# Nine residual chunks turned by VectorE block transposes and DMAs instead of TensorE

## What is computed

```python
def residual_update(x, out, g_post, p_i, w_pp, w_pg):
    x = x + rms_norm(out, g_post)
    return x + (p_i @ w_pp) * jax.nn.sigmoid(x @ w_pg)

def first_block(...):
    out = mixer_a(rms_norm(x, norm_pre[0]), w_in_a[0], w_out_a[0])
    x = residual_update(x, out, norm_post[0], p[0], w_ple_proj[0], w_ple_gate[0])
    kv = shared_kv(x, kv_norm, w_dkv, ...)
    out = mixer_b(rms_norm(x, norm_pre[1]), kv, w_in_b[0], ...)
    return residual_update(x, out, norm_post[1], p[1], w_ple_proj[1], w_ple_gate[1])

def hybrid_layer(h, ...):
    proj = rmsnorm(h, norm1_w) @ w_in
    ...
    h = h + mixed @ w_out
    z = rmsnorm(h, norm2_w) @ mlp_w1
    return h + jnp.square(jax.nn.relu(z)) @ mlp_w2
```

## Time and profile before

| what | us |
|---|---|
| median of 3 runs | 2087.79 |
| lowest and highest run | 2087.12, 2089.4 |
| span of the profiled execution | 2088.3 |
| TensorE matmuls busy in it | 2076.1 |
| VectorE, ScalarE busy in it | 1228.3, 1067.9 |
| GpSimd busy in it | 6.1 |

### The profile page before, as it was taken

One profiled execution on the slowest core, in us unless ns is written; L12 is line 12 of the kernel. 1 busy time (PEld: TensorE's weight loads), 2 busy tenths in 40 slices (PEclk: granted clock), 3 DMA queues, 4 the chain that ended last, 5 costly groups with the idle time before them and its releaser, 6 DMA issues.

```text
span 2088.3 us, 27247 instructions
## 1 busy us (share of the span) xinstructions
PE 2076.1 (99%) x10904; PEld 1779.2 (85%) x10904; DVE 1228.3 (59%) x1506; ACT 1067.9 (51%) x1478; POOL 6.1 (0%) x12
## 2 busy tenths in 40 slices
PE   9999999999999999999999999999999999999998
PEld 8888888888898888888889988888888888888887
DVE  5555556556567767646545557555545645655655
ACT  6444566645566565545564345454434434434443
POOL 0000000000000000000000000000000000000000
PEclk9999999999999999999999999999999999999999
DMA  7666555555556544565545446566666566566664
GB/s 253 187 183 192 178 151 155 188 189 178 189 166 190 159 141 154 177 193 183 187 142 158 136 138 206 184 188 187 195 192 189 190 196 189 187 195 187 192 192 150
DMA packets 211100, 375.16 MB, mean 180 GB/s; under 512 B 13843, under 2 KB 48885, under 8 KB 210582
## 3 DMA queue, kind: packets, MB, share of 16 engines
q1 hardware_dynamic: 210982, 373.52, 57.7%
HBM read 371.38 MB, written 2.10 MB: 179 GB/s over the span
## 4 chain that ended last, share of the span: by engine, by line
PE 99%; ACT 0%; DMA 0%; SPq 0%; DVE 0%; issue 0%; ACTq 0%
PE acc L500 20%; PE acc L502 20%; PE acc L501 20%; PE acc L1023 6%; PE acc L597 3%; PE xb L1023 3%; PE tp L1023 3%; PE acc L1026 3%; PE tp L512 2%; PE acc L916 2%; PE acc L917 2%; PE acc L918 2%; PE tp L597 1%; PE xb L597 1%; PE acc L600 1%; PE tp L1026 1%
## 5 line engine op out<-in xcount | busy, mean ns | idle before, releaser
L1585 DVE TENSOR_TENSOR wlo<-raw,whi 128x1024 fp32r<-128x1024 f32 (+1 forms) x650 | 789.7, 1218 | 704.3 <-ACT whi L1080 703.5
L1080 ACT ACTIVATE whi<-raw 128x1024 fp32r<-128x1024 f32 (+1 forms) x650 | 684.6, 1055 | 789.3 <-PE acc L502 470.2
L500 PE MATMUL acc<-whi,ahi 128*128 128x512 f32 (+1 forms) x976 | 377.9, 387 | 0.0
L502 PE MATMUL acc<-whi,alo 128*128 128x512 f32 (+1 forms) x976 | 374.5, 384 | 0.0
L501 PE MATMUL acc<-wlo,ahi 128*128 128x512 f32 (+1 forms) x976 | 374.0, 383 | 0.0
L500 PEld LDWEIGHTS acc<-whi,ahi 128*128 128x128 f32 x976 | 183.2, 188 | 36.6 <-issue 2.7
L502 PEld LDWEIGHTS acc<-whi,alo 128*128 128x128 f32 x976 | 183.2, 188 | 36.5
L501 PEld LDWEIGHTS acc<-wlo,ahi 128*128 128x128 f32 x976 | 183.4, 188 | 34.3
L1023 PE MATMUL acc<-bT,whi 128*128 128x512 f32 x512 | 160.8, 395 | 0.0
L500 PE MATMUL acc<-whi,bhi 128*128 128x512 f32 x384 | 150.5, 392 | 0.0
L502 PE MATMUL acc<-whi,blo 128*128 128x512 f32 x384 | 149.5, 389 | 0.0
(11 more groups left out here) (366 smaller groups left out, 3089.8 us busy)
## 6 DMA issues: line engine op xcount, KB each, us to landing
raw<-in_mlp_w SPq DMA_DIRECT2D x256, 512.0 KB, 4.3
raw<-in_w_in_a SPq DMA_DIRECT2D x128, 512.0 KB, 4.2
raw<-in_w_ple_gate SPq DMA_DIRECT2D x64, 512.0 KB, 4.4
raw<-in_w_in SPq DMA_DIRECT2D x64, 512.0 KB, 3.8
raw<-in_w_in_b SPq DMA_DIRECT2D x40, 512.0 KB, 4.0
raw<-in_w_out_a SPq DMA_DIRECT2D x32, 512.0 KB, 4.2
raw<-in_w_out_b SPq DMA_DIRECT2D x32, 512.0 KB, 4.4
raw<-in_w_out SPq DMA_DIRECT2D x32, 512.0 KB, 4.4
```

Source lines behind the costliest of these rows:

```text
L500: pe.matmul(o, hi[:, kt, tok], whi[:, slot, wc], start=start, stop=False)
L502: mm = pe.matmul(o, lo[:, kt, tok], whi[:, slot, wc], start=False, stop=stop)
L1080: act.activation(whi[:, u % RING, 0:n], raw[:, u % RING, 0:n], ACT.Copy).then_inc(hi_done, 1)
L1585: dve.tensor_tensor(wlo[:, u % RING, 0:n], raw[:, u % RING, 0:n], whi[:, u % RING, 0:n].bitcast(F32), ALU.subtract).then_inc(lo_done, 1)
```

## The change

Chunks 0 to 2 of x2, x4 and x5 are no longer turned by TensorE. The table `ALONG` is gone. Instead:

1. After the addition that finishes a chunk, VectorE waits for it and turns its 32x32 blocks, each within its 32 partitions, with two transposes of 128x512 (`blocks_turned`, L1676), into the half of `stg` that it has just read, under the name `blk`.
2. SP moves the blocks to their partitions by 16 DMAs of 32 KB (32 partitions, 2 rows of 512 bytes each) from `blk` into the new 4 KB buffer `mov` (`move_blocks`). They stand in four groups of four, behind the loads of step 7 of the next chunk and of the three units after it (`MOVE_AT`). Ahead of the first of a chunk SP waits for `blocks`, and for `split_lo` of the chunk before, since there is only one `mov`.
3. At step 6 of the following chunk ScalarE waits for all 16 (`moved`) and rounds `mov` to the high half (`hi_moved`), one instruction of 1024 or four of 256 with a gain; VectorE makes the low half (`lo_moved`).
4. TensorE waits for `split_lo` instead of `tp_done` where it reads these chunks (`operands`).

The last chunks (batches 6 and 7) stay with TensorE.

```diff
-ALONG = {1: {5: [0, 1]}, 2: {5: [2, 3]}, 3: {5: [4, 5]}}
+BLK = 32
+TURNED_BY = {"x2": "gate0", "x4": "gate1", "x5": "out2"}
+MOVED = [(name, c) for name in TURNED_BY for c in range(3)]
...
+        mov = sb("mov", [P, TT, P // BLK, QT, BLK], F32, region(4 * KB))
+        blk = [sb(f"blk{i}", [P, TT, P // BLK, QT, BLK], F32, stg_at + i * 4 * KB) for i in range(2)]
...
+        MOVE_AT = {S[TURNED_BY[name]].u0 + 8 * (c + 1) + 7 + q: (n, q) for n, (name, c) in enumerate(MOVED) for q in range(P // BLK)}
...
                 sp.dma_start(dst, unit_source(s, j, uu)).then_inc(raw_full[u % RING], 16)
+                if isinstance(j, int) and u in MOVE_AT:
+                    move_blocks(*MOVE_AT[u])
+
+            def move_blocks(n, q):
+                if q == 0:
+                    sp.wait_ge(sem("blocks"), n + 1)
+                    if n:
+                        sp.wait_ge(sem("split_lo"), n)
+                for i in range(P // BLK):
+                    sp.dma_start(mov[q * BLK:(q + 1) * BLK, :, i].rearrange("a t f b -> a t (f b)"),
+                                 blk[block_par(n)][i * BLK:(i + 1) * BLK, :, q].rearrange("a t f b -> a t (f b)")).then_inc(sem("moved"), 16)
...
+            def hi_moved(name, c, dst, gain=None):
+                act.wait_ge(sem("moved"), 256 * (MOVED.index((name, c)) + 1))
+                src = mov[:, :].rearrange("p t i f b -> p f (t i) b")
+                to = dst[:, QT * c:QT * (c + 1), :].rearrange("p f (i b) -> p f i b", b=BLK)
+                ...
+                m.then_inc(sem("split_hi"), 1)
...
+            def blocks_turned(name, c):
+                par = block_par(MOVED.index((name, c)))
+                for t in range(TT):
+                    m = dve.transpose(blk[par][:, t].rearrange("p j f b -> p f j b"),
+                                      x[:, t, c * CH:(c + 1) * CH].rearrange("p (f j b) -> p f j b", f=QT, j=P // BLK))
+                m.then_inc(sem("blocks"), 1)
...
                     dve.tensor_tensor(x[:, :, cols], x[:, :, cols], pp[:, :, cols], ALU.add).then_inc(x_done, 1)
+                    if j < 3:
+                        dve.wait_ge(x_done, 8 * layer + 4 + j + 1)
+                        blocks_turned(x2, j)
...
                 dve.tensor_tensor(x1, x1, acc[p][1][:, :], ALU.add).then_inc(evac_dve, 1)
+                if j < 3:
+                    dve.wait_ge(evac_dve, c + 1)
+                    blocks_turned("x5", j)
...
-                along(S["out2"], j, los("x5", x5hi, x5lo, GC["norm2"], ALONG[j]) if j else los("mixed", ahi, alo, mixed_gain, MIXED_LATE))
+                along(S["out2"], j, {6: [lambda j=j: lo_moved("x5", j - 1, x5hi, x5lo, GC["norm2"])]} if j else los("mixed", ahi, alo, mixed_gain, MIXED_LATE))
```

More of the change, by code:

```diff
@@ L287, in build @@
         x_done = sem("x_done")
-        order = [("gcol", 1), ("x0", 8), ("p", 2), ("norms", 1), ("ogA", 8), ("x1", 8), ("x2", 8), ("ckv", 2), ("kr", 1),
-                 ("cq", 2), ("uq", 16), ("ogB", 8), ("x3", 8), ("x4", [0, 1, 2, 3, 4, 5]), ("meta", 1),
+        order = [("gcol", 1), ("x0", 8), ("p", 2), ("norms", 1), ("ogA", 8), ("x1", 8), ("x2", [6, 7]), ("ckv", 2), ("kr", 1),
+                 ("cq", 2), ("uq", 16), ("ogB", 8), ("x3", 8), ("meta", 1),
                  ("x4", [6, 7]), ("rsb", 1), ("qdec", 2), ("kend", 2),
-                 ("vT", 4), ("kvM", 1), ("mixed", 8), ("x5", 8)]
+                 ("vT", 4), ("kvM", 1), ("mixed", 8), ("x5", [6, 7])]
         whole = ("gcol", "norms", "kr", "uq", "rsb", "qdec", "kend", "vT", "kvM")
@@ L486, in product, with operands @@
                     if need:
-                        pe.wait_ge(tp_done, BATCH[need, uu][0] + 1)
+                        operands(need, uu)
                     unit(u + uu, bank, hi, lo, uu * s.kt, s.kt, s.cols, uu == 0, uu == s.units - 1, r)
+            def operands(name, uu):
+                if (name, uu // 2) in MOVED:
+                    pe.wait_ge(sem("split_lo"), MOVED.index((name, uu // 2)) + 1)
+                else:
+                    pe.wait_ge(tp_done, BATCH[name, uu][0] + 1)
             def unit(u, bank, hi, lo, kt0, n, cols, first, last, r=0):
@@ L708, in post @@
                 for j in range(4):
-                    hooks = turns(x2, ALONG[j]) if j else turns(x1, X1_LATE)
+                    hooks = {} if j else turns(x1, X1_LATE)
                     if layer and j == 3:
@@ L986, in _ @@
             for j in range(4):
-                product(S["out2"], j, ahi, alo, need=None if j else "mixed", hooks=turns("x5", ALONG[j]) if j else turns("mixed", MIXED_LATE))
+                product(S["out2"], j, ahi, alo, need=None if j else "mixed", hooks={} if j else turns("mixed", MIXED_LATE))
             def up(q, j):
@@ L1122, in hi_batch @@
                 m.then_inc(tp_hi, 1)
+            def hi_moved(name, c, dst, gain=None):
+                act.wait_ge(sem("moved"), 256 * (MOVED.index((name, c)) + 1))
+                src = mov[:, :].rearrange("p t i f b -> p f (t i) b")
+                to = dst[:, QT * c:QT * (c + 1), :].rearrange("p f (i b) -> p f i b", b=BLK)
+                if gain is None:
+                    m = act.activation(to, src, ACT.Copy)
+                else:
+                    for k in range(QT):
+                        g = gain + QT * c + k
+                        m = act.activation(to[:, k], src[:, k], ACT.Copy, scale=gcol[:, g:g + 1])
+                m.then_inc(sem("split_hi"), 1)
             def squares(norm, j, src, junk=None):
@@ L1307, in last_squares @@
                         squares(norms, j - 1, x)
-                    hooks = join({4: [last_squares]}, his(x2, x4hi if layer else ahi, gain, ALONG[j])) if j else his(x1, ahi if layer else bhi, None, X1_LATE)
+                    hooks = join({4: [last_squares]}, {6: [lambda j=j: hi_moved(x2, j - 1, x4hi if layer else ahi, gain)]}) if j else his(x1, ahi if layer else bhi, None, X1_LATE)
                     along(s, j, join(hooks, {6: [meta_in], 7: [meta_root]}) if layer and j == 3 else hooks)
@@ L1628, in lo_batch, with lo_moved @@
                 m.then_inc(tp_done, 1)
+            def blocks_turned(name, c):
[4 more added lines that the diff above has]
+                m.then_inc(sem("blocks"), 1)
+            def lo_moved(name, c, hi, lo, gain=None):
+                dve.wait_ge(sem("split_hi"), MOVED.index((name, c)) + 1)
+                src = mov[:, :].rearrange("p t i f b -> p f (t i) b")
+                from_hi, to = (a[:, QT * c:QT * (c + 1), :].rearrange("p f (i b) -> p f i b", b=BLK) for a in (hi, lo))
+                if gain is None:
+                    m = dve.tensor_tensor(to, src, from_hi.bitcast(F32), ALU.subtract)
+                else:
+                    for k in range(QT):
+                        g = gain + QT * c + k
+                        m = dve.scalar_tensor_tensor(out=to[:, k], in0=src[:, k], scalar=gcol[:, g:g + 1], in1=from_hi[:, k].bitcast(F32),
+                                                     op0=ALU.mult, op1=ALU.subtract)
+                m.then_inc(sem("split_lo"), 1)
             def copy_batch(name, f, dst, r=0):
```

9 lines of the change are left out of this document (6 added, 3 removed).

## The result

The changed kernel takes **2101.65 us** (median of 4 runs, 2099.89 to 2102.91) where the kernel before takes 2087.78 beside it: ratio 1.0067, 95% interval 1.0053 to 1.0080. It is 13.9 us slower; 7.8 us faster was forecast, and the range ended at 2086.0. Its profiled execution spans 2098.1 us (in every run shown here the time is the span plus 1.8).

A forecast was written before the change was run, and what follows sets the result against it. TensorE, busy 2076.1 of 2088.3 us, was taken as the bound: 2088.3 - 8.1 for the removed transposes + 0.3 for a stall at q2 = 2080.5, less 0.5 from span to median: 2080.0 us, range 2078.5 to 2086.0.

The forecast's parts named there:

- Nine groups at 0.90 us: On TensorE: nine groups of 8 transposes removed, each adding 0.89 to 0.90 us to a chunk, 8.1 us saved.
- Rival 3: On VectorE: block transposes of 4-byte data run at a quarter of the rate, 2.76 us each; 2094.4 us, chance 0.04.
- rival 4: On the DMA engines: moves are served one after another, 1.7 us each, costing 148 us; 2228 us, chance 0.01.
- rival 5: TensorE wasn't the bound, and the 8.1 us turn into waits for weight splits; 2087.8 us, chance 0.03.
- The path from a landing to the next split TensorE needs: ScalarE's moved split, a weight split and sigmoid, then VectorE's chunk end and first split: some 8.8 us from landing.
- the three signs: TensorE waiting for weight splits near gate chunk ends, a move's issue over 0.68 us, or a block transpose over 1.65.
- rival 2: On SP: moves issue at the start's 0.91 us, landing 7.8 later and stalling 37 us; 2117 us, chance 0.07.
- rival 1: On SP: moves partly late at 0.55 to 0.68 us an issue; 2084.0 us, 2081 to 2088 at the ends, chance 0.10.
- Issue: On SP's queue: each move occupies it 0.42 us, weight loads 0.4; the last moves land 17.5 us after the chunk's start.
- 6 L - 17.3: Stall sum over six gate chunks when moves land L us late, beyond 3.6; four have 3.6 free, others 2.4 and 0.5.
- 5.2 us free: In out2, three times: lateness of the moves that costs nothing, its chunk end being 1.6 us shorter than a gate's.
- ckv and q2: Chunks ahead of these have least free time, 2.4 and 0.5 us; stalls (L - 2.4) + (L - 0.5) for landings L late.

The follow-up runs named there:

- e1: The changed kernel with the moves left out, the splits reading the block-transposed data where VectorE wrote it (turned chunks wrong): 2079.14 us, ratio 0.9952 to the kernel before.
- e6: The change for chunks 0 and 1 of each product only, chunk 2 turned by TensorE as before, moves on SP: 2088.45 us, ratio 1.0005 to the kernel before.
- e5: The change with moves issued by GpSimd and, in layer 1's last gate chunk, the meta tokens' work ahead of the moved split: 2080.67 us, ratio 0.9966 to the kernel before.

## Why the prediction was wrong

**Right.** Nine groups at 0.90 us: e1 gives 8.5 for 8.1, and 21.76 us a chunk. A block transpose was taken at 0.69 us from a VectorE addition of the same shape; here is its row (ns min/median/max):

```profile
L1676 DVE STREAM_TRANSPOSE blk<-x x18: 668/692/712, 529.8 to 1362.0; 128x512 f32<-128x512 f32 x18
```

Its time was as said, and it was free where nothing is late (e1); in the change it is part of each late chunk end, as the prediction's path had it. Rival 3 falls, as do rival 4 (moves overlap: four issued in 2.51 us land 2.9 after each) and rival 5. The path from a landing to the next split TensorE needs, 8.8 us, measured 8.35 (571.74 to 580.09, where TensorE starts). Of the three signs that would prove me wrong one came: waits for weight splits near gate ends. The other two did not (a move's issue over 0.68 us, a block transpose over 1.65). The outcome was rival 2's, slower (given 0.07), but at an issue price from rival 1's range, 0.55 to 0.68 us (given 0.10), whose times ended at 2088. So neither rival had both: the kernel was slower at a price at which every sum of the prediction still made it faster or the same.

**Wrong, the step that failed.** "Issue [...] I take 0.42, since at most some two loads are outstanding here." The number was drawn from gain rows of 8 KB and less at the start, with 0.91 as the other end; measured 0.60, 0.63 in a row, and 0.59 for a load among moves. The overlap that was counted on failed with it: the moves were not there when ScalarE asked for them. Put into the same chain: 16 x (0.63 - 0.42) + 3 x 0.19 = 3.9 us later, 21.4 instead of 17.5, and 21.3 was measured in gate0's second chunk. The chain was right and its price wrong. That the two agree to 0.1 is in part luck: SP was done 19.2 us after the chunk's start (545.32 - 526.13), 4.7 later than forecast, with 0.7 more in the first group of four and the small gaps between groups, and the last landing came 2.1 us behind that, not 3.0 as forecast. In e6's trace the same sixteen moves were there only after 23.2 us (549.07 - 525.89).

**Wrong, the formula behind it.** At a landing 3.8 late, 6 L - 17.3 gives 5.5 us and 2085. There were 14.7 us of stalls, so the price alone does not explain the sign. Three terms were missing:
- *Lateness carried over.* Each chunk was reckoned from a fresh start. But the load ahead of the next moves waits for a split behind the late chunk end, so gate0's landings go from 21.3 to 23.85 us after the chunk's start. Of the stalls, 6.1 us stand in gates and out2 behind chunks 0 and 1, where L = 3.8 gave 0.2 each in the four gate chunks and nothing in out2.
- *up0.* For out2 I took 5.2 us free, from the first weight split TensorE would miss. TensorE needs something earlier there: the copy at L1583, which follows the last chunk's work on ScalarE. It cost 4.0 us, where nothing was charged.
- *What a stall costs beyond itself.* From the second chunk of gate0 to the end the change takes 2098.1 - 526.1 = 1572.0 us, e1 2077.7 - 527.8 = 1549.9, so 22.1 are lost (the start before it differs by up to 3 us from run to run). 14.7 are the nine stalls. 2.3 are their restarts: a wait counts from the modelled end of the last matmul, 0.39 us after its start, where the next could start after 0.23, and the first step behind it takes 0.33; 9 x 0.26. 4.5 are the clock, as the same matmuls in both traces drift apart: 1.7 behind 1036.94 and 2.8 behind 1383.11. The sum is 21.5 of 22.1.

ckv and q2 came near the formula, 1.4 and 3.3 us at L = 3.8 against 2.1 (0.72 and 1.42) and 2.5 measured, but not for its reasons alone. ckv's data came 24.9 us after its chunk would have started without a stall (594.56 - 569.65), and TensorE was late itself by then; and what q2 waited for was the meta tokens' split, not the weight split that I had reckoned with.

**One that did no harm, by luck.** I came from the span to the median by taking 0.5 us off. In truth a time is the span plus 1.8, and the profiled execution was of the upper group of times, some 2.3 above the median. Against the median the sum is 2087.8 - 8.1 + 0.3 = 2080.0 as well.

**The rule I set aside.** The Trainium skill (DMA: Bandwidth & Descriptors, Rules for kernel authors) counts a transfer under 64 KB as mostly overhead. I weighed it for the landing and found the overhead overlapped. It does overlap there, but the part of it that SP pays doesn't: 16 issues are 10 of the 21.8 us of a chunk, on the queue that also feeds the weights.

## What to carry to other kernels

Price an added DMA by what it holds on its issuing queue, 0.6 us here for 16 to 64 KB alike, and count what that queue carries besides; here many small moves did best on a queue that nobody needed. Then follow the first consumer's engine past its wait, to everything that TensorE needs from behind it, the bank releases as well as the splits, and carry each chunk's lateness into the next. Where the saved work is real but something is late, changing who issues and where the wait stands (e5, 2080.67) can bring back nearly all of it.
